# First norm of a one-layer hybrid block: inversions of three blocks' roots behind the last block's sums of squares, and the first tile evicted in two parts

## The reference, cut to what matters

```python
def rms_norm(x, g):
    xf = x.astype(jnp.float32)
    y = xf * lax.rsqrt(jnp.mean(xf * xf, axis=-1, keepdims=True) + EPS)
    return (y * g.astype(jnp.float32)).astype(x.dtype)

h = rms_norm(x, attn_norm_g[i])
proj = h @ w_in[i]
q, k, v, z, xbc, dt_raw = jnp.split(proj, splits, axis=-1)
```

## Time and profile before

| | us |
|---|---|
| median of three runs | 3297.41 |
| the three runs | 3290.4, 3297.41, 3297.6 |
| profiled execution, its own time | 3292.06 |
| its span | 3290.3 |
| TensorE busy | 3142.9 (96%) |
| VectorE busy | 1553.2 (47%) |
| ScalarE busy | 818.0 (25%) |

### The profile page before, as it was taken

How to read it: one execution, slowest core, us unless ns; L and a number is a source line. 1 busy time by engine, 2 the same in 40 slices (tenths; PEclk the granted TensorE clock), 3 DMA queues, 4 the chain that set the end, 5 groups by cost and what they waited for, 6 DMA issues and landing times. The chain is left out here.

```text
span 3290.3 us, 38000 instructions
## 1 busy us (share of the span) xinstructions
PE 3142.9 (96%) x15525; PEld 2462.4 (75%) x15590; DVE 1553.2 (47%) x1562; ACT 818.0 (25%) x1148; POOL 227.6 (7%) x182
## 2 busy tenths in 40 slices
PE   7999999968999997999899999999999999999899
PEld 5788888745665655788688888888887788788687
DVE  6325552146656544442754455444545532532743
ACT  5221221113443533210411111111111422421421
POOL 0000000003343441000000000000000000000000
PEclk9999999978999998999999999999999999999899
DMA  4441222247667454443211111111011634433542
GB/s 143 148 142 58 76 76 77 77 119 175 157 198 186 133 139 151 157 133 115 91 51 51 51 51 51 51 51 51 34 43 64 224 128 153 173 126 119 159 144 67
DMA packets 231005, 361.39 MB, mean 110 GB/s; under 512 B 39885, under 2 KB 124877, under 8 KB 222573
## 3 DMA queue, kind: packets, MB, share of 16 engines
q1 hardware_dynamic: 227182, 339.88, 33.2%
q0 software_dynamic: 3712, 19.96, 1.6%
HBM read 262.37 MB, written 96.94 MB: 109 GB/s over the span
## 5 line engine op out<-in xcount | busy, mean ns | idle before, releaser
L90 PE MATMUL up_ps<-up_h_hi,up_w_hi 128*128 128x512 f32 x1408 | 550.1, 391 | 7.3 <-DVE up_h_lo L1806 7.3
L92 PE MATMUL up_ps<-up_h_hi,up_w_lo 128*128 128x512 f32 x1408 | 548.5, 390 | 0.0
L91 PE MATMUL up_ps<-up_h_lo,up_w_hi 128*128 128x512 f32 x1408 | 548.5, 390 | 0.0
L90 PE MATMUL inp_ps<-inp_h_hi,carry_q 128*128 128x512 f32 x896 | 352.6, 393 | 12.1 <-DVE inp_h_lo L189 9.3
L91 PE MATMUL inp_ps<-inp_h_lo,carry_q 128*128 128x512 f32 x896 | 350.1, 391 | 0.0
L92 PE MATMUL inp_ps<-inp_h_hi,carry_k_two 128*128 128x512 f32 x896 | 349.7, 390 | 0.0
L90 PEld LDWEIGHTS up_ps<-up_h_hi,up_w_hi 128*128 128x128 f32 x1408 | 264.9, 188 | 63.7 <-issue 8.8
L91 PEld LDWEIGHTS up_ps<-up_h_lo,up_w_hi 128*128 128x128 f32 x1408 | 264.9, 188 | 55.5 <-issue 0.7
L92 PEld LDWEIGHTS up_ps<-up_h_hi,up_w_lo 128*128 128x128 f32 x1408 | 264.8, 188 | 55.2
L1951 DVE TENSOR_TENSOR carry_squares<-up_ps,carry_rows 128x2048 f32<-128x2048 f32 x42 | 96.3, 2292 | 420.6 <-PE up_ps L92 420.2
L90 PE MATMUL down_banks<-down_a_hi,down_w_hi 128*128 128x512 f32 x704 | 276.7, 393 | 15.0 <-DVE down_a_lo L2177 8.8
(11 more groups left out here) (318 smaller groups left out, 4536.8 us busy)
## 6 DMA issues: line engine op xcount, KB each, us to landing
carry_room<-in_w_up_dram SPq DMA_DIRECT2D x42, 512.0 KB, 6.0
act<-carry_room SPq DMA_DIRECT2D x21, 1024.0 KB, 4.5
carry_room<-act SPq DMA_DIRECT2D x7, 2816.0 KB, 13.6
down_a_second<-act SPq DMA_DIRECT2D x7, 2816.0 KB, 18.4
carry_room<-cum_rows SPq DMA_DIRECT2D x16, 1024.0 KB, 6.0
carry_room<-x SPq DMA_DIRECT2D x8, 2048.0 KB, 9.2
carry_room<-in_w_in_dram SPq DMA_DIRECT2D x26, 512.0 KB, 6.0
xbc<-carry_room SPq DMA_DIRECT2D x12, 1024.0 KB, 5.7
```

The costliest lines, as they stand in the source:

```text
L90: pe.matmul(out, w_hi, x_hi, start=first, stop=False)
L91: pe.matmul(out, w_hi, x_lo, start=False, stop=False)
L92: return pe.matmul(out, w_lo, x_hi, start=False, stop=last)
```

## The change

VectorE no longer inverts the root of block n - 1 between the low parts and the sums of squares of block n. The inversions of blocks 0, 1 and 2 stand in a row behind the sums of squares of block 3. The eviction of tile 0 is taken out of the loop over the tiles, goes ahead of L462 and L464, and is made in two parts: the first 1536 tokens behind the three inversions, then the inversion of block 3, then the last 512 tokens. Only the second part raises `evacuated`. The first part waits for `mm_done` 1 and for three inversions, the second for four. No other engine's list changes.

```diff
@@ Norm.vector @@
-        def invert(n):
-            dve.wait_ge(self.rooted, n + 1)
-            blk = self.rstd[:, n * 512:(n + 1) * 512]
-            dve.reciprocal(blk, blk).then_inc(self.inverted, 1)
-
         for n in range(NB):
...
             if n == 0:
                 self.low_weights(dve, 1, w_hi, w_lo, whi_done)
-            else:
-                invert(n - 1)
             dve.wait_ge(self.squared, n + 1)
...
-        invert(NB - 1)
-        dve.wait_ge(self.inverted, NB)
+        for n in range(NB - 1):
+            self.invert(dve, n)
+
+    def invert(self, dve, n):
+        dve.wait_ge(self.rooted, n + 1)
+        blk = self.rstd[:, n * 512:(n + 1) * 512]
+        dve.reciprocal(blk, blk).then_inc(self.inverted, 1)
@@ in_projection, VectorE @@
             norm.vector(dve, w_hi, w_lo, whi_done)
+
+            def evacuate_first():
+                dve.wait_ge(mm_done, 1)
+                dve.wait_ge(norm.inverted, NB - 1)
+                dve.tensor_tensor(stage[0][:, 0:SEQ - 512], ps[0][:, 0:SEQ - 512], norm.rstd[:, 0:SEQ - 512], ALU.mult)
+                norm.invert(dve, NB - 1)
+                dve.wait_ge(norm.inverted, NB)
+                dve.tensor_tensor(stage[0][:, SEQ - 512:], ps[0][:, SEQ - 512:], norm.rstd[:, SEQ - 512:], ALU.mult).then_inc(evacuated, 1)
+
+            evacuate_first()
             dve.wait_ge(wd_hi_s, 1)
...
-                evacuate(t, b, stage[b])
+                if t > 0:
+                    evacuate(t, b, stage[b])
```

## The result

The changed kernel takes 3297.94 us (median of 22 runs) against 3292.41 us (22 runs of the kernel before beside them): a ratio of 1.0017, interval 1.0011 to 1.0024, so 5.5 us more. Run twice more beside the experiments it gave 1.0023 (1.0013 to 1.0033) and 1.0029 (1.0017 to 1.0040). The profiled execution took 3302.36 us with a span of 3300.6 us.

The account below looks back on a forecast made before the run. TensorE, busy 96% of the span, was taken to bound the kernel. A 3.3 us later eviction plus 0.6 us of clock made 3.9 us on a base of 3297.41: 3301.3 us, range 3292 to 3307.

Parts of the forecast that it names:

- Block 1's inversion was hidden: VectorE, block 1: sums of squares start at 29.50 with or without the inversion, so removing it gains nothing.
- the 0.75: VectorE, block 2: without the inversion the sums start at 40.78, 0.75 us earlier, and TensorE's wait at 45.07 shrinks.
- Three inversions near 54.1, 57.3 and 60.6: VectorE behind block 3's sums: three inversions at 3.26 us start to start, no idle time in front, ending near 64.0.
- the further 0.2 us that the prediction names for chaining: VectorE's chained inversions: by the skill's pipe-drain rule the eviction would end some 0.2 us later still.
- The eviction 3.3 us later: VectorE's eviction of tile 0 ends at 69.8 rather than 66.5, delaying the square and TensorE's sums by head.
- the term that I mis-sized: TensorE's clock after the longer 6.5 us pause: between 2.9 us added and 1.8 gained, taken as 0.6 us added.
- the old loss: Eight half-clock matmuls from 74.2 to 77.7 in tile 2's product before the change, costing 1.8 us at most.
- rival (a): TensorE's clock falls on the sums by head and again on the product: 6.2 us more, 3303.6 us; chance 0.25.
- The total of 3.9 us: Whole kernel: 3.3 us later eviction plus 0.6 us clock, giving 3301.3 us; chance 0.45.
- Rival (c): Not slower: three fewer slow stretches from 680 to 1320 us give back 5.4 us, 3295.9 us; chance 0.16.
- Rival (b): TensorE's longer pause takes in the whole slow time: 1.5 us more, 3298.9 us; chance 0.12.
- Rival (d): VectorE's inversions stay hidden, fitting into the 3.44 us of idle time: no change, 3297.4 us; chance 0.02.

Follow-up runs that it names:

- the kernel where the clock was held up: Changed kernel plus 22 unread matmuls on TensorE in the pause before the sums by head; ratios to the kernel before 1.0016, 1.0014 and 1.0017.
- two inversions against three: Changed kernel with block 0's inversion back in its old place, leaving two behind the last sums; ratio 1.0006 to the kernel before.

## Why the prediction was right

The direction, the place and the chain were right. Point by point:

- Block 1's inversion was hidden: its sums start at 29.65 after, 29.50 before, the 0.15 being the trace's later start. Block 2's held the sums back: TensorE's pause there fell from 3.08 to 2.40 us, 0.68 of the 0.75.
- Three inversions near 54.1, 57.3 and 60.6: they began at 54.27 and took 9.77 us together. Chained, they took less than three times 3.34 us, so the further 0.2 us that the prediction names for chaining did not come. The first part of the eviction cost 1.76 us, as worked out; the fourth inversion began at 65.83 (65.7), and the eviction ended at 69.89 (69.8).
- The eviction 3.3 us later: 3.4 in the two traces, 3.1 us at the product's start, with the 0.7 taken off, in the kernel where the clock was held up.
- The clock was the term that I mis-sized. I took the middle between 1.8 us gained and 2.9 lost, 0.6 us. The profile shows 2.9 lost (6.49 against 3.59 us) with the old loss still there; the three profiles of the changed kernel have 6.49, 6.50 and 6.00 us. That was rival (a), which I gave 0.25 although the nearest rows had 4.4 and 5.8 us of slow work behind pauses hardly longer. (their first lines stand below the list); I should have gone by them. Rival (a)'s sum, 6.2 us, is what the stage shows. The old loss, which I put at 1.8 us at most, is 1.6: 10.00 us from the product's start to the next sums by head with it, 8.4 without.
- The total of 3.9 us was measured as 5.5 in the first comparison and 7.6 and 9.5 in the others. The predicted 3301.3 us stands 3.4 us over the measured 3297.94 for another reason: its base. The three runs shown first had a median of 3297.41, the 22 runs one of 3292.41; a base of three runs that lie 7 us apart was worth no better. The base was 5.0 us too high and the change put 1.6 us too low, so that the total came near is in part luck.
- Rival (c), slow stretches elsewhere giving the loss back, did not come: the one profile had 4 us more of them, and no comparison came out faster. Rival (b) needed the slow work to end within the pause, and it did not. Rival (d) was wrong, as two inversions against three showed.

In the kernel before, the slow work behind the pauses of 7.3 and 8.4 us begins with these lines:

```profile
1578.55 0.76 PE L90 MATMUL up_ps<-up_h_hi,up_w_hi 128*128 128x512 f32 x1 [7.28 <-DVE up_h_lo L1806]
...
2553.27 0.79 PE L90 MATMUL down_banks<-down_a_hi,down_w_hi 128*128 128x512 f32 x1 [8.38 <-DVE down_a_lo L2177]
```

## What to carry to other kernels

Before an operation is moved out of the way, ask what its engine would do in its place: two of these three inversions stood mostly or wholly in waits, and nobody waited for the sums behind the third. In a row at the end, those that the idle time there no longer held cost their 3.3 us in full: from three to two the pause falls from 6.34 to 3.09 us. A part of an operation split off gains what there is of waiting ahead of its last input, so split what can lie in that wait and move no more into it than it holds. And price a longer pause of TensorE with the clock, from the slow work behind pauses of like length in the same trace, and look at the next pause behind it too.

## What I had not expected of the hardware

The slow stretch on the product of tile 2 hangs on a pause further ahead. The pause right ahead of that product is 2.05 us in all 13 profiles. In the six in which TensorE had also paused 2.40 us or more ahead of the sums by head, some eight matmuls of the product ran at half clock, and the next sums by head started 9.97 to 10.03 us behind its start; in the seven in which that pause was 0.6 us or less, none did, and it took 8.38 to 8.41 us. The sums by head themselves ran at full clock behind the pause of 2.40 us (3.59 us), and in part at half clock behind those of 3.09 us (5.29 us) and of 6.30 to 6.39 us (6.00 to 6.50 us).

A pause of the same length does not always bring the clock down. Ahead of the sums of block 2 TensorE pauses 2.4 or 3.1 us in every kernel here. In the traces of the kernel before, of the changed kernel and of one repetition of it, the two matmuls behind took 1.12 or 1.13 us, in all the others about 2.07 us, at half clock:

```profile
45.04 2.07 PE L220 MATMUL inp_ps<-inp_squares,inp_ones 128*128 128x512 f32 x2 [2.40 <-DVE inp_squares L193]
```

That is the kernel with the unread matmuls, whose list up to there is the changed kernel's. The pause of 6.3 us brought the clock down in all three profiles of the changed kernel. Such stretches, met or not, may be much of why runs of one kernel lie up to 18 us apart here; that was not tried.
